# Latent attention and its output projection in one stage, output products two steps later than in the first version of it, weight splits spread

## The reference, cut to what matters

```python
def chunk_causal_attention(q, k, v, pos, scale):
    ...
        logits = jnp.einsum('bqhd,bshd->bhqs', qb, k, ...) * scale
        visible = key_chunk[:, None, None, :] <= (pb // CHUNK)[:, None, :, None]
        p = jax.nn.softmax(jnp.where(visible, logits, NEG_INF), axis=-1)
        return jnp.einsum('bhqs,bshd->bqhd', p.astype(v.dtype), v)
...
def mla_mixer(u, pos, w_in, q_norm_g, w_q_up, kv_norm_g, w_kv_up, w_out):
    ...
    out = chunk_causal_attention(q, k, v, pos, (C_NOPE + C_ROPE) ** -0.5)
    return out @ w_out
```

## Time and profile before

| | us |
|---|---|
| median of three runs | 1551.37 |
| lowest and highest | 1549.98, 1555.17 |
| profiled execution: device time | 1555.45 |
| profiled execution: span of the trace | 1553.6 |
| TensorE matmul busy | 1443.9 (93%) |
| VectorE busy | 1157.6 (75%) |
| ScalarE busy | 847.7 (55%) |

### The profile page before, as it was taken

How to read it: one execution, slowest core, us unless ns; L and a number is a source line. 1 busy time by engine, 2 the same in 40 slices (tenths; PEclk the granted TensorE clock), 3 DMA queues, 4 the chain that set the end, 5 groups by cost and what they waited for, 6 DMA issues and landing times. The chain is left out here.

```text
span 1553.6 us, 23401 instructions
## 1 busy us (share of the span) xinstructions
PE 1443.9 (93%) x8807; PEld 1243.5 (80%) x8807; DVE 1157.6 (75%) x2067; ACT 847.7 (55%) x1612; POOL 0.2 (0%) x4
## 2 busy tenths in 40 slices
PE   3999998997988999989999899899998999999988
PEld 3878888996867888878888786688886888798766
DVE  6888878877679888789888756796667656647564
ACT  1545445563456545465544556565455676666653
POOL 0000000000000000000000000000000000000000
PEclk9999999998999999999999999999999999999999
DMA  9989876740036888659887342477555446437200
GB/s 370 339 311 343 304 257 193 240 138 1 1 127 229 300 318 308 207 174 330 311 282 245 111 142 96 149 248 240 179 189 169 129 138 215 111 99 227 82 1 28
DMA packets 197382, 306.16 MB, mean 197 GB/s; under 512 B 10551, under 2 KB 158998, under 8 KB 197270
## 3 DMA queue, kind: packets, MB, share of 16 engines
q1 hardware_dynamic: 196464, 304.40, 57.5%
q10 hardware_dynamic: 806, 0.26, 0.1%
HBM read 303.59 MB, written 1.05 MB: 196 GB/s over the span
## 5 line engine op out<-in xcount | busy, mean ns | idle before, releaser
L915 PE MATMUL bank<-u_hi_lo,w_hi 128*128 128x512 f32 x1344 | 472.7, 396 | 10.2 <-DVE arena L981 10.2
L914 PE MATMUL bank<-u_hi_lo,w_lo 128*128 128x256 f32 x1176 | 327.9, 279 | 0.0
L970 DVE TENSOR_TENSOR w_lo<-weight_ring,w_hi 128x1024 fp32r<-128x1024 f32 x264 | 307.9, 1219 | 17.9 <-ACT w_hi L940 17.2
L915 PEld LDWEIGHTS bank<-u_hi_lo,w_hi 128*128 128x128 f32 x1344 | 246.1, 188 | 62.7 <-DVE arena L981 14.5
L940 ACT CAST w_hi<-weight_ring 128x1024 fp32r<-128x1024 f32 x264 | 260.5, 1047 | 39.8 <-DMA weight_ring<-in_ffn_w_gate_dram 26.9
L914 PEld LDWEIGHTS bank<-u_hi_lo,w_lo 128*128 128x128 f32 x1176 | 221.7, 189 | 7.3
L837 PE MATMUL bank<-src_hi,wp_hi 128*128 128x256 f32 (+2 forms) x672 | 191.6, 299 | 2.0 <-ACT src_hi L434 1.5
L837 PE MATMUL bank<-src_hi,wp_lo 128*128 128x256 f32 (+2 forms) x672 | 180.8, 284 | 0.0
L837 PE MATMUL bank<-src_lo,wp_hi 128*128 128x256 f32 (+2 forms) x672 | 180.7, 284 | 0.0
L353 DVE SCALAR_TENSOR_TENSOR zT<-weight_ring,silu_c,zT 128x1024 f32<-128x1024 f32 x126 | 161.5, 1282 | 4.6 <-DMA weight_ring<-in_mod_w_dram 1.9
L837 PE MATMUL bank<-w_hi,hidden_hi 128*128 128x512 f32 x352 | 140.6, 399 | 0.0
(11 more groups left out here) (382 smaller groups left out, 2313.8 us busy)
## 6 DMA issues: line engine op xcount, KB each, us to landing
weight_ring<-in_mod_w_dram SPq DMA_DIRECT2D x72, 1024.0 KB, 6.7
weight_ring<-in_ffn_w_gate_dram SPq DMA_DIRECT2D x44, 1024.0 KB, 5.9
weight_ring<-in_ffn_w_up_dram SPq DMA_DIRECT2D x44, 1024.0 KB, 5.5
weight_ring<-in_ffn_w_down_dram SPq DMA_DIRECT2D x44, 1024.0 KB, 8.2
weight_ring<-in_hyb_w_in_dram SPq DMA_DIRECT2D x16, 1024.0 KB, 8.1
weight_ring<-in_w_in_e_dram SPq DMA_DIRECT2D x16, 1024.0 KB, 8.0
weight_ring<-in_w_in_o_dram SPq DMA_DIRECT2D x13, 1024.0 KB, 6.5
weight_ring<-in_hyb_w_out_dram SPq DMA_DIRECT2D x4, 1024.0 KB, 4.8
```

The lines of the kernel that those rows point to most:

```text
L914: nc.tensor.matmul(bank[:, 0:SEQ], w[1], u[:, 0:SEQ], start=False, stop=False, skip_group_check=True)
L915: last = nc.tensor.matmul(bank[:, :], w[0], u, start=kt == 0, stop=kt == KT - 1, skip_group_check=True)
L970: nc.vector.tensor_tensor(part_view(wl, n, part), raw, part_view(wh, n, part).bitcast(F32), ALU.subtract).then_inc(w_lo.sem, w_lo.up())
```

## The change

`mla` is moved behind the class `Steps` without an edit, but for its last lines, which no longer run `attention` and `out_proj` one after the other but one stage with both, `attend_and_project`. `Steps` is made with `wide` = 99, so that all 16 units use the same two banks for their logits, and takes its own room for the transposed probabilities (the place used by the later layers holds this layer's values). Output products are placed at given steps: those of weight pieces 0 to 3 from step 10 on, two token halves each, those of pieces 4 to 7 with the first token half at steps 18 to 21 and with the second after the loop. ScalarE makes the high parts of the weights at steps 1, 3, 5, 7, 12, 14, 16, 18, VectorE their low parts one step later; VectorE scales the residual rows at steps 9 and 13; the attention result is split at steps 8, 12, 16 and 19.

```diff
-            attention([Pair(heads[2 * p:2 * p + 2], same_bias(bias), uT[:, p, :], causal=False) for p in range(8)])
-            out_proj(D["mla_w_out"][0], uT, 0, x_rows_of=(3, 1))
+            top = arena.at
+            arena.at = keep
+            steps = Steps([Pair(heads[2 * p:2 * p + 2], same_bias(bias), uT[:, p, :], causal=False) for p in range(8)], 99, (),
+                          arena.take(2 * 4 * SEQ))
+            arena.at = top
+            attend_and_project(steps, D["mla_w_out"][0], 3)
...
-            def __init__(self, pairs, wide, wide_in):
+            def __init__(self, pairs, wide, wide_in, turned_in=None):
...
-                self.pT = zT.rearrange("p k t -> p (k t)").rearrange("p (b h q) -> p b h q", b=2, h=4)
+                self.pT = (zT.rearrange("p k t -> p (k t)") if turned_in is None else turned_in) \
+                    .rearrange("p (b h q) -> p b h q", b=2, h=4)
...
+        def attend_and_project(steps, w_out, rows_of):
...
+            tiles = [rows_tile(w_out, 2 * m * P) for m in range(n_out)]
+            x_rows = ln_rows(rows_of)
+            first_at = (10, 14, 18, 20)
+            parts_at = {first_at[m] + 2 * k + a: (m, k, a) for m in range(2) for k in range(2) for a in range(TT)}
+            parts_at.update({18: (2, 0, 0), 19: (2, 1, 0), 20: (3, 0, 0), 21: (3, 1, 0)})
+            split_at = {1: 0, 3: 1, 5: 2, 7: 3, 12: 4, 14: 5, 16: 6, 18: 7}
+            scale_at = {9: 0, 13: 1}
+            mix_of = {8: 0, 12: 1, 16: 2, 19: 3}
...
+            @block.scalar
...
+                def split_hi(n):
+                    tile = tiles[n // 2]
+                    act.wait_ge(loaded[tile.slot], tile.need)
+                    if n >= 4:
+                        act.wait_ge(w_used.sem, w_used.base + n - 3)
+                    nc.scalar.copy(wh[:, n % 4, :], tile.w[:, n % 2, :]).then_inc(w_hi.sem, w_hi.up())
...
+                for i in range(steps.count):
+                    steps.act(act, i)
+                    if i in split_at:
+                        split_hi(split_at[i])
+                    if i in mix_of:
+                        m = mix_of[i]
+                        act.wait_ge(out_taken.sem, out_taken.base + 2 * m + 2)
+                        nc.scalar.copy(mh[:, 2 * m:2 * m + 2, :], uT[:, 2 * m:2 * m + 2, :]).then_inc(mix_hi.sem, mix_hi.up())
...
+            @block.vector
...
+                def split_lo(n):
+                    tile = tiles[n // 2]
+                    dve.wait_ge(w_hi.sem, w_hi.base + n + 1)
+                    nc.vector.tensor_tensor(wl[:, n % 4, :], tile.w[:, n % 2, :], wh[:, n % 4, :].bitcast(F32),
+                                            ALU.subtract).then_inc(w_lo.sem, w_lo.up())
+                    if n % 2:
+                        tile.free(w_lo)
...
+                for i in range(steps.count):
+                    steps.dve(dve, i)
+                    if i - 1 in split_at:
+                        split_lo(split_at[i - 1])
+                    if i in scale_at:
+                        scale_rows(dve, x_rows, scale_at[i])
+                    if i in mix_of:
+                        m = mix_of[i]
+                        dve.wait_ge(mix_hi.sem, mix_hi.base + m + 1)
+                        nc.vector.tensor_tensor(ml[:, 2 * m:2 * m + 2, :], uT[:, 2 * m:2 * m + 2, :],
+                                                mh[:, 2 * m:2 * m + 2, :].bitcast(F32), ALU.subtract) \
+                            .then_inc(mix_lo.sem, mix_lo.up())
...
+            @block.tensor
...
+                for i in range(steps.count + 2):
+                    if i < steps.count:
+                        steps.pe(pe, i)
+                    if i in parts_at:
+                        m, k, a = parts_at[i]
+                        if k + a == 0:
+                            pe.wait_ge(mix_lo.sem, mix_lo.base + m + 1)
+                        if a == 0:
+                            pe.wait_ge(w_lo.sem, w_lo.base + 2 * m + k + 1)
+                        for h in range(2):
+                            last = part(m, k, a, h)
+                        if a or m >= 2:
+                            last.then_inc(w_used.sem, w_used.up())
+                for h in range(2):
+                    for m in (2, 3):
+                        for k in range(2):
+                            last = part(m, k, 1, h)
+                    last.then_inc(tokens_out.sem, tokens_out.up())
```

More of the change, by code:

```diff
@@ new lines, in attend_and_project, with _, part @@
+        def attend_and_project(steps, w_out, rows_of):
+            room = arena_room()
+            mh, ml = (t[:, :].rearrange("p (k t) -> p k t", k=KT) for t in halves(room, "mix", KT * SEQ))
+            wh, wl = (t[:, :].rearrange("p (s n) -> p s n", s=4) for t in halves(room, "wp", 4 * KT * P))
+            room.close()
+            n_out = KT // 2
+            tiles = [rows_tile(w_out, 2 * m * P) for m in range(n_out)]
[6 more added lines that the diff above has]
+            mix_of = {8: 0, 12: 1, 16: 2, 19: 3}
+            assert steps.count == 20
+            @block.scalar
+            def _(act):
+                act.wait_ge(stage_done.sem, stage_done.base)
+                def split_hi(n):
[12 more added lines that the diff above has]
+                        nc.scalar.copy(mh[:, 2 * m:2 * m + 2, :], uT[:, 2 * m:2 * m + 2, :]).then_inc(mix_hi.sem, mix_hi.up())
+                act.drain().then_inc(stage_done.sem, stage_done.up())
+            @block.vector
+            def _(dve):
+                dve.wait_ge(stage_done.sem, stage_done.base)
+                def split_lo(n):
[17 more added lines that the diff above has]
+                            .then_inc(mix_lo.sem, mix_lo.up())
+                dve.drain().then_inc(stage_done.sem, stage_done.up())
+            @block.tensor
+            def _(pe):
+                pe.wait_ge(stage_done.sem, stage_done.base)
+                def part(m, k, a, h):
+                    n = 2 * m + k
+                    tok = slice(a * P, (a + 1) * P)
+                    return product(y_bank(a, h), (mh[:, n, tok], ml[:, n, tok]),
+                                   (wh[:, n % 4, half_row(h)], wl[:, n % 4, half_row(h)]), n == 0, n == KT - 1)
+                for i in range(steps.count + 2):
[5 more added lines that the diff above has]
+                            pe.wait_ge(mix_lo.sem, mix_lo.base + m + 1)
+                        if a == 0:
+                            pe.wait_ge(w_lo.sem, w_lo.base + 2 * m + k + 1)
[8 more added lines that the diff above has]
+                    last.then_inc(tokens_out.sem, tokens_out.up())
+                pe.drain().then_inc(stage_done.sem, stage_done.up())
+            for sig in (w_hi, w_lo, w_used, x_ready, stage_done, logits_ready, biased, probs_ready, rows_ready, probsT_ready,
+                        probsT_copied, pv_done, out_taken, mix_hi, mix_lo):
+                sig.close()
+            y_done[:] = [(w_used.sem, w_used.count)] + [(tokens_out.sem, tokens_out.count - i) for i in (1, 0)]
```

291 lines of the change are left out of this document (145 added, 146 removed).

## The result

| | before | changed |
|---|---|---|
| median of 18 runs | 1551.53 us (1546.40 to 1555.28) | 1555.77 us (1548.96 to 1563.19) |
| ratio, 95% interval | | 1.0035, [1.002, 1.005] |
| span of the profiled execution | 1553.6 us | 1553.5 us |
| stage, first logits to end of last product | 62.62 us | 66.27 us |
| mean granted clock of timed runs | 0.977 (29 runs of it, timed with the experiments) | 0.974 (18 runs) |

What follows compares the result with a forecast made beforehand. TensorE, 93% busy, was taken to bound the kernel. Winning handover, dip and overlap, less a longer thin part, waits and interleaving, took the stage from 62.6 to 61.4: 1551.37 - 1.2 = 1550.2 us, range 1547.0 to 1554.0.

Steps and rivals of the forecast that it cites:

- A dip of 3 us costs up to 1.5 and one of 6 up to 3. I take none as likeliest: Thin first steps of the new stage: a fall to 1.2 GHz possible, none assumed, 3 us kept for the range.
- the walk: Step-by-step sum of durations over the joined attention and output stage: 61.4 us against 62.6, so 1.2 us less.
- the two pauses of rows 6: Earlier trace: after 2.4 us at 1480.7 the clock stood at 0.50; after 3.2 us at 1509.7 it stayed 1.00.
- attention kept 1.00 for all of its 37 us, of which 8 were free: Attention in the kernel before: TensorE held full clock despite free time, the argument against a lasting clock fall.
- the slow rival: Thin steps 0 to 9: the clock falls and stays, adding 10 us, which gives 1560; chance 0.10.
- The rule that spoke against the change: Skill's warning on brief idles between groups: thin steps would run at 1.2 GHz, stage some 71 us instead of 61.4.
- step 14 waits: Step 14's reading queues behind step 13's low part and scaling, 5.1 us: logits 15 at 41.5 instead of 40.4.
- the signs of being wrong: Clock 0.50 in the stage's first 25 us, products awaiting low parts, stage under 58 or over 66, or feed-forward length moved.
- cover works better than walked: Steps 0 to 9 take 21.7 us, TensorE never waits from step 10: stage 57.5, whole 1546.3; chance 0.15.
- It doesn't do what it says: Output products pile up behind the loop because splits are late: 62.6 less the handover; chance within "same", 0.75.
- handover: Stage boundary from last value product to first output product: 2.2 us removed, with the 1.6 us clock dip behind it.
- Loads at nothing: Output-weight tiles come free earlier, same tiles issued by stage end: cost nothing, bounds 0 and 0.6 us if late.

Runs made afterwards that it cites:

- fill: The changed kernel with 14 idle matmuls, results never read, in TensorE's pauses of steps 0 to 9; stage 61.81 us, ratio 0.9996 to the kernel before.
- again: The changed kernel as it is, profiled in a second execution; stage 66.31 us.
- fill2on: The changed kernel with idle matmuls only in the pauses of steps 2 to 9; stage 62.52 us, ran once.
- onepair: The kernel before, stages still apart, with all its attention logits in one pair of banks; stage 67.91 us, ratio 1.0018 to the kernel before.
- thin2: The kernel before with only logits 1 and 2 made to wait for the reading of the unit before them; stage 64.88 us, ran once.
- scale17: The changed kernel with VectorE's second scaling of residual rows at step 17 instead of 13; stage 65.78 us, ratio 1.0017 to the kernel before.
- fill01: The changed kernel with idle matmuls only after steps 0 and 1, three each; stage 63.24 us, ran once.
- twin: The changed kernel with a second pair of logits banks in steps 0 to 9; stage 59.70 us, ratio 0.9978 to the kernel before.
- twin1: The changed kernel with a second pair of banks for logits 1 alone; stage 61.46 us, ran once.
- early: The changed kernel with two pairs of logits banks in steps 0 to 9, output products a step sooner, splits, scalings and low parts moved; 1546.47 us, ratio 0.9964.

## Why the prediction was wrong, point by point

- **The failed step is the clock's:** "A dip of 3 us costs up to 1.5 and one of 6 up to 3. I take none as likeliest". The term was put at 0 and measured +4.9 us against the walk (66.27 - 61.4), or 4.5 against fill, the same loop at full clock: 13.6 us at 0.50. The price per microsecond was right (4.9 / 13.6 = 0.36, bound 0.5); the length was not, and I had weighed the two pauses of rows 6 as one for and one against. Both follow a single pause in otherwise full work, and such a pause goes either way with the same work: the pause of 2.47 us at 1510, which had no dip in the kernel before, is in the changed kernel's profile too (the two lines below), and there the clock fell for 3.4 us. So the two answers that I weighed told nothing either way. The new stage has two pauses of 1.4 and 1.3 us in a row with 0.7 us of work between, and all profiles that begin this way (changed, again, fill2on, onepair, thin2, scale17) dipped at about 4 us; the six that don't (before, fill, fill01, twin, twin1, early) kept 1.00 there. The pause at 1510, in the kernel before and in the changed one:

```profile
1512.88 0.66 PE L2772 MATMUL bank<-tables_sb,arena 128*128 128x128 f32 x4 [2.47 <-DVE arena L2864]
```

```profile
1511.46 1.12 PE L2504 MATMUL bank<-tables_sb,arena 128*128 128x128 f32 x4 [2.47 <-DVE arena L2596]
```

- **"attention kept 1.00 for all of its 37 us, of which 8 were free"**, the reason given against the slow rival, took the free share of the whole for what matters. In fill01 the 11.2 us behind the start had 1.9 free at a clock of 1.00. What the change took away was the pair of steps back to back at the very start (2.10 us of weight loads in the first 3, then 1.36), and thin2, which takes away nothing else, dipped.
- **The rule that spoke against the change deserved more.** The Trainium skill, in "TensorE: Matmul & The Clock Gate", section "A second HAM failure mode: psum-queue depth-cycling", names short idles between groups that cycle through banks. The trace here agrees on the idles: pauses of 1.9 us at most in the first 27 us, and a clock of 0.50 for 10.2 of them. It is not the cycling: before and twin cycle through two pairs of banks at the start and kept 1.00, thin2 cycles through the same two with two waits added and dipped. The rival built on it (1560) had the mechanism and the sign, and failed in size: the clock rose again by itself at 951 while the thin steps went on, so 4.9 us were lost, not 10.
- **The walk was right,** to 0.7 us. With the clock held it forecasts 61.4 against 61.81 (fill), 59.7 against 59.70 (twin), 56.0 against 56.66 (early). Its parts show in the changed kernel: loop 2.0 to 2.1, step 14 waits, and no matmul-free 2 us before the first output product (the longest is 1.66). That no clock of 0.50 would stand there was wrong: the second dip, up to 968.1, reaches over that product's start at 967.93. Of the signs of being wrong, two came: 0.50 within the first 25 us, and a stage over 66.
- **The rival "cover works better than walked"** is excluded by the same numbers: fill wins nothing beyond the 61.4, and its logits 10 start 23.9 us after the first, walked 23.6, where the rival has 21.7.
- **"It doesn't do what it says"** is excluded too: handover gone, products between steps.
- **Loads at nothing: right.** SP issues as forecast; the stretches behind the stage moved by 0.6 and 0.4 us, less than a dip. The changed kernel's issues, the first and last of the ring's in the stage, and the next:

```profile
951.82 0.37 SPq L3817 DMA_DIRECT2D weight_ring<-in_mod_w_dram  x1
...
994.18 0.58 SPq L3817 DMA_DIRECT2D weight_ring<-in_ffn_w_up_dram  x1
...
1016.39 0.37 SPq L3817 DMA_DIRECT2D weight_ring<-in_mod_w_dram  x1
```

- **The sum redone:** 1551.37 - 1.2 + 4.9 = 1555.1, measured 1555.77. With the term sized the working gives the result to 0.7 us; the interval of the ratio spans 3.1 to 7.8 us, so that closeness is in part luck.

## What to carry to other kernels

A change that makes TensorE take turns with another engine, by one buffer less, is best costed twice: by the walk, and with the clock at half from the first thin steps on. Look at the start of the stage, not at its mean, and keep two steps' work ready there with a second pair of banks, or fill the pauses with idle matmuls. Where two profiled spans agree and the timed runs don't, compare stretch by stretch.

## What the runs showed that I had not expected

- Two steps with pauses of 1.4 and 1.3 us at the start were followed by a dip in six profiles of six, and in none of the six without them; and adding 14 idle matmuls made a stage 4.5 us shorter.
- The dips inside the stage lasted 3.4, 6.8 or 10.2 us, in every kernel, and cost the stage 0.33 (fill2on) to 0.54 us (fill01) for each at 0.50, with the walk's error in it; 0.5 is what a stretch bound by TensorE alone would lose.
- The dip behind the handover, there before, was absent in onepair and thin2 though the pause of 2.20 us was kept. It needn't come from their edits: in work that no edit touches, dips differ too. At 34 us from the start of the span six of the twelve profiles have 6.8 us at 0.50 and six none; at 1200 it's 10.2 us in nine and 6.8 in three.
- A kernel's own runs differ by 14 us (1548.96 to 1563.19), and over the 18 runs time and mean granted clock go together with a correlation of -0.89 (-0.15 in fill's 12 runs and -0.14 in twin's, so it isn't general): dips elsewhere come and go (fill2on's only run, 1558.25, has one of 20.5 us at 892, ahead of the stage). A single execution therefore says nothing on totals here, and only the stage was read from it.
- Open: that every timed run of the changed kernel has both dips was not seen. Two profiled executions have them, and its mean clock of 0.974 over 18 runs, against 0.977 to 0.979 in before, fill, twin and early, fits. That of onepair, 0.978, does not fit a dip of 10.2 us in each of its runs, and neither does its ratio.
